# Expert stage of a three-block model: the product with the gates moved from ScalarE to VectorE and one group later, and fewer of the additions of fetched rows on VectorE

## The reference, cut to what matters

```
scores  = queries . sub_keys                      # two sets of 128 keys for each head
top 16 of each set, top 16 of their 256 sums      -> expert numbers, gates = softmax(best scores)
for each token, for each of its 128 (head, expert) pairs:
    dot  = <h, down[expert]>                      # 1024 products
    y   += gates * gelu(dot) * up[expert]         # 1024 products
out = x + gate_row * y
```

## Time and profile before

| | |
|---|---|
| median of 3 runs | 3574.54 us (3574.5 to 3578.73) |
| the profiled execution, its own time | 3574.5 us |
| its span | 3572.6 us |
| granted TensorE clock, mean | 0.929 |
| PE busy | 3002.4 us (84%), 11946 instructions |
| DVE busy | 2174.7 us (61%), 4024 instructions |
| ACT busy | 1381.8 us (39%), 2846 instructions |
| POOL busy | 622.5 us (17%), 540 instructions |
| fetches (queue q0) | 536.90 MB, 73728 packets |
| weights and the rest (queue q1) | 251.69 MB |

### The profile page before, as it was taken

How to read it: one execution, slowest core, us unless ns; L and a number is a source line. 1 busy time by engine, 2 the same in 40 slices (tenths; PEclk the granted TensorE clock), 3 DMA queues, 4 the chain that set the end, 5 groups by cost and what they waited for, 6 DMA issues and landing times.

```text
span 3572.6 us, 34443 instructions
## 1 busy us (share of the span) xinstructions
PE 3002.4 (84%) x11946; PEld 2081.4 (58%) x11946; DVE 2174.7 (61%) x4024; ACT 1381.8 (39%) x2846; POOL 622.5 (17%) x540
## 2 busy tenths in 40 slices
PE   5989999798777889999898886888878567777777
PEld 4868888587555668887677753456546322223222
DVE  6655443676555444442354679989768979755555
ACT  3233222443444442222471355674433333333333
POOL 0000000000000000000000013334443355444442
PEclk9999999899888999999899987889989789999999
DMA  6534444243111324443321457889999799999998
GB/s 222 187 129 136 142 143 134 81 137 106 37 46 36 106 88 142 142 142 100 107 83 36 189 205 301 302 343 373 389 413 396 261 412 422 422 421 422 421 421 336
DMA packets 147549, 797.82 MB, mean 223 GB/s; under 512 B 16305, under 2 KB 18481, under 8 KB 81713
## 3 DMA queue, kind: packets, MB, share of 16 engines
q0 software_dynamic: 73728, 536.90, 37.2%
q1 hardware_dynamic: 69840, 251.69, 20.7%
q10 hardware_dynamic: 3808, 7.02, 0.5%
HBM read 793.46 MB, written 2.10 MB: 223 GB/s over the span
## 4 chain that ended last, share of the span: by engine, by line
PE 54%; DVE 19%; DMA 17%; ACT 5%; issue 4%; POOL 0%; another core or an unknown queue 0%; DVEq 0%; SPq 0%; ACTq 0%; POOLq 0%
PE psum L153 54%; DMA tail<-in_experts,tail 16%; DVE tail L187 5%; DVE tail L182 3%; DVE tail L170 2%; ACT arena L164 2%; DVE arena L182 2%; ACT L164 2%; DVE tail L193 1%; DVE tail L190 1%; ACT tail L164 1%; DVE tail L196 1%; DVE region L170 1%; DVE tail L205 1%; PE psum L158 1%
## 5 line engine op out<-in xcount | busy, mean ns | idle before, releaser
L153 PE MATMUL psum<-tail,arena 128*128 128x256 f32 (+2 forms) x3460 | 1244.6, 509 | 307.0 <-ACT arena L164 274.6
L153 PE MATMUL psum<-rounded,rounded 128*128 128x512 f32 x5496 | 1293.7, 396 | 39.9 <-DVE rounded L182 27.2
L153 PEld LDWEIGHTS psum<-rounded,rounded 128*128 128x128 f32 x5496 | 1036.8, 190 | 279.9 <-issue 56.4
L153 PEld LDWEIGHTS psum<-tail,arena 128*128 128x128 f32 x3460 | 659.4, 201 | 842.9 <-issue 784.8
L216 POOL DMA_INDIRECT tail<-in_experts,tail x512 | 602.3, 1176 | 1781.0 <-DVE tail L199 862.8
L187 DVE CUSTOM_DVE_ANT_0 tail<-tail 128x1024 f32<-128x1024 f32 x512 | 622.8, 1223 | 311.4 <-DMA tail<-in_experts,tail 310.3
L164 ACT ACTIVATE tail<-tail 128x1 f32<-128x1 f32 (+1 forms) x1056 | 266.5, 252 | 830.0 <-DVE tail L187 792.6
L170 DVE TENSOR_TENSOR rounded<-arena,rounded 128x1024 fp32r<-128x1024 f32 (+2 forms) x285 | 316.5, 1111 | 346.7 <-ACT rounded L164 346.5
L164 ACT ACTIVATE rounded<-arena 128x1024 fp32r<-128x1024 f32 (+2 forms) x317 | 291.9, 939 | 446.1 <-DVE arena L170 238.9
L153 PE MATMUL psum<-arena 128*128 128x1 f32 (+3 forms) x792 | 196.9, 373 | 86.8 <-ACT arena L164 47.7
L164 ACT ACTIVATE arena<-psum 128x256 f32<-128x256 f32 (+2 forms) x210 | 97.9, 482 | 419.8 <-PE psum L153 413.5
(11 more groups left out here) (82 smaller groups left out, 1549.8 us busy)
## 6 DMA issues: line engine op xcount, KB each, us to landing
arena<-in_ada SPq DMA_DIRECT2D x136, 512.0 KB
arena<-in_fin SPq DMA_DIRECT2D x88, 512.0 KB
arena<-in_win SPq DMA_DIRECT2D x56, 512.0 KB
arena<-in_fout SPq DMA_DIRECT2D x32, 512.0 KB
arena<-in_mxbc SPq DMA_DIRECT2D x32, 512.0 KB
arena<-in_pq SPq DMA_DIRECT2D x32, 512.0 KB
arena<-in_ain SPq DMA_DIRECT2D x24, 512.0 KB
arena<-in_mz SPq DMA_DIRECT2D x16, 512.0 KB
```

Source lines behind the costliest of these rows:

```text
L153: return self.e.matmul(o, a, b, start=start, stop=stop, skip_group_check=skip)
```

## The change

The product with the gates leaves ScalarE. VectorE does it with a tensor_tensor of 128x1 (`dve_gate`), and it stands after the dots of the next group: dots of g, gate of g - 1, own addition of g - 1. ScalarE keeps the Gelu (`act_gelu`), and its diagonal of g - 1 now stands behind the Gelu of g. `own_add` takes s % 4 = 1 from 24 on for n < 256 (26 of each of the blocks 0 and 1, 48 fewer together), and for the later blocks what it took before.

```
         def own_add(n):
             s = n % 128
-            return 24 <= s < 124 and (s % 2 == 1 if n < 256 else s % 16 == 9)
+            return s >= 24 and (s % 4 == 1 if n < 256 else s % 16 == 9)
...
-        def act_gate(e, c, grp):
-            n = 128 * c + grp
-            d = dots[n % 8]
-            e.wait_ge(*g_dot.at(n))
+        def dve_gate(e, c, grp):
+            n = 128 * c + GG * grp
+            d = dots[(n // GG) % 8]
+            e.wait_ge(*g_gelu.at(n))
+            e.wait_ge(*gate_ok.at(c))
+            e.tt(d, d, gates[c % 2][:, GG * grp:GG * grp + GG], ALU.mult).then_inc(*g_act.tick((c, grp)))
+
+        def act_gelu(e, c, grp):
+            n = 128 * c + GG * grp
+            d = dots[(n // GG) % 8]
+            e.wait_ge(*g_dot.at(n + GG - 1))
             e.act(d, d, ACT.Gelu).then_inc(*g_gelu.tick(n))
-            e.wait_ge(*gate_ok.at(c))
-            e.wait_ge(*g_gelu.at(n))
-            e.act(d, d, ACT.Copy, scale=gates[c % 2][:, grp:grp + 1]).then_inc(*g_act.tick((c, grp)))
...
         def act_experts(e, ranks):
...
-                act_gate(e, c, grp)
-                act_diag(e, c, grp)
+                act_gelu(e, c, grp)
+                if g:
+                    act_diag(e, *ALL_GROUPS[g - 1])
...
+            act_diag(e, *ALL_GROUPS[-1])
...
         def dve_experts(e, ranks):
...
                 dve_dots(e, c, grp)
                 if g:
+                    dve_gate(e, *ALL_GROUPS[g - 1])
                     dve_add(e, *ALL_GROUPS[g - 1])
...
+            dve_gate(e, *ALL_GROUPS[-1])
             dve_add(e, *ALL_GROUPS[-1])
```

## The result

The changed kernel takes 3593.86 us (median of 7 runs, 3591.1 to 3606.76) where the kernel before takes 3574.54. The ratio is 1.0063, 95% interval 1.0051 to 1.0075; it is taken over all 24 runs of the changed kernel, whose median is 3597.03. The profiled execution has a span of 3594.6 us, 22.0 more than before.

The account below looks back on a forecast made before the run. DMA bounds the kernel from 3091 us on; before, engines take turns, with VectorE full by a hair in the inverse. Terms -8 + 27.5 + 5 + 8 + 6 + 3 + 3.5 = +45 on 3574.5 give 3620 us, range 3582 to 3652.

Parts of the forecast that it names:

- (5): Stretches bound by TensorE: more additions there cost +6, and +3 where TensorE and VectorE alternate (2256.7 to 2408.2).
- (2): Inverse's six levels: odd additions await late diagonals and hold up the next step's products; 4.6 us each, +27.5 us.
- (1): VectorE's work in the first and last stretch where it is full: fewer own additions, more gate products, -8 us.
- (4): Block 1's first steps, groups 127 to 147: odd additions wait for late diagonals, delaying the next products; +8 us.
- (6): Ends of the blocks and last group: the final additions come later, after the last dots; together +3.5 us.
- (3): Three pairs ahead of the levels (91, 95, 99): same wait, but steps depend less on each other; +5 us.
- (A): Whole kernel: relieving VectorE, the busiest engine in the inverse, wins and makes it faster, 3556 us; chance 0.09.
- (B): Inverse and after: waits fall into time idle anyway under saturated DMA; within 0.2%, 3575 us; chance 0.06.
- (C): TensorE idles in the levels, so its clock drops too and the loss grows, 3647 us; chance 0.2.
- (D): Block 0 ahead of the inverse: each gate on VectorE waits for a Gelu, no relief, 3665 us; chance 0.05.
- if the gates wait for Gelu: Sign in the changed profile, VectorE's gates waiting for ScalarE's Gelu, that would show the forecast wrong; no size given.

Follow-up runs that it names:

- the last version: Kernel before, VectorE's own additions by stretch: s % 8 = 1 in groups 24-47 and 196-231, all odd in 91-125, one in four elsewhere: 3542.13 us, 0.9903.
- one in eight: Kernel before, with VectorE's own additions cut to s % 8 = 1 in blocks 0 and 1 (13 of each): 3551.94 us, ratio 0.9945.

## Why the prediction was right in its sign and wrong in its size

In spans, +22.0 against the sum's +45. Term (5) was 20 us too high, (2) 8, and (1), (4) and (6) 6 together; (3) was 8 too low, and some 3 us belong to no term. One by one:

(1) VectorE's work, -8: measured in the two stretches -9.4 (87.40 to 84.70 and 129.50 to 122.80). Right, though both its prices were off. A product lasts 0.15 us by its row, but the dots behind it start 0.07 later (2511.06 to 2511.13); where its own addition follows, it is 0.19 (2519.73 to 2519.92). Half of each makes the 0.13 measured with every second group an own addition. An own addition less was worth 1.0 us (6.0 for 6) and 1.1 (10.0 for 9), not 1.20, and that with a higher clock on TensorE in both stretches (0.70 to 0.80, 0.79 to 0.89).

(2) The levels, +27.5: +19.7. The mechanism is shown: additions stand ahead of the products behind late diagonals (an order of TensorE's list in which they stand behind the products took all but 3.5 us of it away). Its working was good until the products start, 5.10 computed and 4.89 measured. What failed is the next line, "the 16 products take 3.85 until VectorE can use them". VectorE's d step takes them in halves: its first half starts 1.98 us behind the first product, and the second finds its products 0.50 after. The step is over 4.97 us behind the products' start, not 3.85 + 2.40 = 6.25, which is 1.28 us a level. The list of VectorE before, printed in the section on the change, says so: it waits for `inv_products` twice. The timeline before couldn't, since there VectorE was late anyway. The sum also took six levels of 10.56 us, where the last took 8.96 and grew by only 2.4; against that, the two levels with the lower clock took 1.06 us more each. A second thing was not in the sum: the even group's addition is late as well, from 0.75 on. It hides behind the odd one's wait here, but where only even groups are added on TensorE it costs 0.7 to 0.8 us a level at a clock of 1.00 and 2.3 to 2.5 in the levels at 0.87, together 9.5 and 11.7 for six, and I hadn't seen it until giving the odd ones back left +9.3.

(3) The pairs ahead of the levels, +5: +12.9, or 4.3 a pair, as much as I took for a level. "Their steps depend on each other less" was a guess that these pairs didn't bear out; the value lies just under the upper bound of 14. Products of TensorE hold 38.9% of the chain of waits there, 1.8% once the odd additions stand behind the step, and with those additions back on VectorE +2.2 us are left. The clock is part of it in a measure that no run separates: in the second and third of the pairs it was 0.78 and 0.72, where before it was 0.87 and 0.82.

(4) Block 1's first steps, +8: +5.4, and +4.9 with the late diagonal alone. Right in kind, and a third less than forecast.

(5) The stretches in which TensorE is the bound, +9: measured -7.0 in groups 44 to 87 (11 additions moved, not 10) and about -4 in the two others (-2.7 and -1.4 in 148 to 163 and 184 to 195). This is the step that failed most, by some 20 us. I read TensorE's busy share as work: 129.20 of 151.5, 37.83 of 39.2. The chain of what released what says otherwise. Its shares by line, before, in groups 60 to 87 (a view that I hadn't read for single stretches):

```profile
by line: DVE tail L182 28.1%; DVE tail L187 26.9%; ACT arena L164 9.2%; ACT tail L164 8.3%; PE psum L153 7.8%; ACT L164 6.7%; issue 6.6%; DVE tail L176 3.9%; DVE arena L177 2.9%; DVEq L148 0.0%
```

The same groups with the own additions moved, and the gate not:

```profile
by line: PE psum L153 55.8%; DVE tail L182 10.5%; ACT arena L164 8.9%; DVE tail L187 7.6%; ACT L164 7.0%; ACT tail L164 2.7%; DVE tail L176 2.7%; DVE arena L177 2.6%; issue 2.4%; PE psum L158 0.2%; DVEq L148 0.0%
```

VectorE held the path for over half the time while TensorE was busy 80.9 of 96.2 us. With 7 additions less on VectorE the stretch fell to 91.9 us, and TensorE has the larger share. That share alone proves little: two other kernels with the same own additions in these groups, the changed one (90.1 us) and the last version (91.5), have TensorE at 5.8% and 21.3%, so no single share says which engine is the bound there. What shows that TensorE wasn't the bound before is that the stretch got shorter with more work on it, and what shows that it then nearly is, that one in eight makes it longer again. The clock moved too, from 0.89 before to 0.98 and 1.00, and no run tells that part from VectorE's relief. The Trainium skill, "Perfetto Trace Analysis", section "Identifying the Most-Contended Engine", says that TensorE's matmul busy share doesn't show how near it is to its limit and points to its useful arithmetic and its weight loads instead. The trace agrees: weight loads are busy 57.23 of those 96.2 us, and 65.06 of 95.00 where TensorE was the bound.

In groups 184 to 195 the fetches hold the path before (62.7%, DMA share 1.01 in 2682.2 to 2721.4), and the additions lie beside them. In 148 to 163 TensorE does hold it (79.9%), as I had taken; that they didn't get longer stays open, but they are 2.1 us shorter with the gate alone, without one addition moved.

(6) The ends, +3.5: from group 340 to the end +1.7, as computed for the last group (+1.6). The ends of blocks 0 and 1 don't stand out from their neighbours.

What no term had: some 3 us more, spread mostly over groups 0 to 23, 164 to 183 and 232 to 255, where most runs differ by 1 to 2 us; it stays open.

The rivals: (A), that relief of VectorE wins, was the better half of the truth. Alone it gives -20 us, the figure worked out for it (58 - 38), though that figure had the products in it, and the agreement is luck; its condition "If nothing of TensorE's list waited" is what the other half of the change breaks. (B)'s saturated DMA didn't hide the levels: its share fell from 1.00 to 0.85. (C) had the clock the wrong way round for the whole: the granted mean rose from 0.929 to 0.941, with the busier TensorE of groups 24 to 87 (0.71 to 0.80, 0.89 to 0.99). In the levels its mechanism is there: the clock fell from 1.00 to 0.96, worth 2.1 us in two of them, and with the late diagonal alone it fell in four of the six. (D), that each gate waits for the Gelu, needs the gate ahead of the dots: there VectorE waited 7.5 us in groups 24 to 47 and 26.4 in 48 to 91. Where the change puts it, these are at most 0.4 and 7.1. It waited in few places, and groups 0 to 23, with the longest wait of 10.8 us, got 0.9 us longer; the prediction's sign of being wrong, "if the gates wait for Gelu", came in part, but it is not where the time went.

## What to carry to other kernels

Ask of each stretch which engine its chain of waits runs through, not which one is busy: a TensorE busy 84% of the span had 23.7% of the chain from 1800 us on, the fetches 33.0%. Then move a little work and see whether the stretch gets shorter, since the shares of two engines that are nearly even say little. Moving work and moving the moment at which a neighbour gets its input are two changes; run them apart, since here one was worth -20 us and the other +30. Look at the granted clock of the single period before putting a wait down to the order alone. On an engine that works in order, an item goes behind whatever can start without it, and where a consumer takes its input in halves, a wait is as long as the first half.

## What the hardware showed that was not expected

A 128x1 product on VectorE lasts 0.15 us in its row, but the next instruction started 0.07 us behind its start when it didn't need the result (2511.06 to 2511.13), and 0.19 when it did (2519.73 to 2519.92). The same lists of instructions gave levels of 11.40 us at a granted clock of 1.00 and of 13.06 at 0.87, one behind the other in one execution. More work on TensorE went with a higher granted clock: in groups 24 to 47 it was 0.70 before, 0.80 with the own additions moved and 0.83 in the last version, whose stretch is 9.7 us shorter. How much of the gain is the clock's and how much VectorE's relief no run here separates.
